# Longer rows for gates and values in memory, and loads asked for one stage ahead, in a two-layer attention kernel

## The reference, cut to what matters

```python
def _mixer_swa(h, positions, w_in, sinks):
    proj = h @ w_in
    q, k, v, z = jnp.split(proj, [MIX_WIDTH, MIX_WIDTH + SWA_KV, MIX_WIDTH + 2 * SWA_KV], axis=-1)
    q = _rope(q.reshape(B, S, N_HEADS, HEAD_DIM), positions)
    k = _rope(k.reshape(B, S, SWA_KV_HEADS, HEAD_DIM), positions)
    o = _banded_gqa(q, k, v, SWA_WINDOW, sinks).reshape(B, S, MIX_WIDTH)
    return o * jax.nn.silu(z)

def _mixer_mla(h, positions, w_in, q_norm, kv_norm, w_uq, w_ukv):
    cq, ckv, kr, z = jnp.split(h @ w_in, [...], axis=-1)
    q = (_rmsnorm(cq, q_norm) @ w_uq)      # nope 64 and rope 32 per head
    kv = (_rmsnorm(ckv, kv_norm) @ w_ukv)  # key 64 and value 64 per head
    o = _mla_attention(q_nope, q_rope, k_nope, k_rope, v)
    return o * jax.nn.silu(z)

for i in range(DEPTH):
    y = mixers[i % N_MIXERS](x, ...) @ w_out[i]
    x = _layernorm(DEEPNORM_ALPHA * x + y, ln_g[i], ln_b[i])
    x = x + jax.nn.sigmoid(x @ pe_gate[i]) * (p[i] @ pe_proj[i])
```

## Time and profile before

| what | value |
|---|---|
| median of 3 runs | 3186.99 us (3185.19 to 3197.34) |
| the profiled execution, its own time | 3190.66 us |
| its span | 3188.8 us |
| mean granted TensorE clock | 0.968 |
| PE busy | 2962.2 us (93%) |
| DVE, ACT, POOL busy | 1895.7, 1627.8, 1430.5 us |
| DMA packets, bytes | 311302, 540.87 MB |

### The profile page before, as it was taken

How to read it: one execution, slowest core, us unless ns; L and a number is a source line. 1 busy time by engine, 2 the same in 40 slices (tenths; PEclk the granted TensorE clock), 3 DMA queues, 4 the chain that set the end, 5 groups by cost and what they waited for, 6 DMA issues and landing times. The chain is left out here.

```text
span 3188.8 us, 40986 instructions
## 1 busy us (share of the span) xinstructions
PE 2962.2 (93%) x13536; PEld 2324.3 (73%) x13536; DVE 1895.7 (59%) x2696; ACT 1627.8 (51%) x2830; POOL 1430.5 (45%) x1154
## 2 busy tenths in 40 slices
PE   7999977887999999999987599999999999799998
PEld 6888875565788788777765377777777777588876
DVE  3544213443378864555653478787787787347875
ACT  3111213566435544444554177777777777544553
POOL 0022003555222540000653078888888888522353
PEclk9999998999999999999999599999999999899999
DMA  5255339885997675554899832432533432499674
GB/s 171 77 121 128 109 92 203 181 178 136 286 289 242 211 241 181 172 169 157 292 355 322 220 72 70 101 98 71 128 71 89 108 72 54 120 307 282 226 233 151
DMA packets 311302, 540.87 MB, mean 170 GB/s; under 512 B 48000, under 2 KB 135680, under 8 KB 302912
## 3 DMA queue, kind: packets, MB, share of 16 engines
q1 hardware_dynamic: 222176, 387.82, 43.5%
q10 hardware_dynamic: 88928, 150.64, 15.7%
HBM read 361.79 MB, written 176.29 MB: 169 GB/s over the span
## 5 line engine op out<-in xcount | busy, mean ns | idle before, releaser
L2454 POOL TENSOR_TENSOR mla_pl<-mla_p,mla_ph 128x512 fp32r<-128x512 f32 (+3 forms) x640 | 707.2, 1120 | 205.4 <-ACT mla_p L2325 197.7
L1455 PE MATMUL end_bank<-end_xh,end_whi 128*128 128x512 f32 x1808 | 719.0, 398 | 61.4 <-DVE end_xl L1706 28.7
L1456 PE MATMUL end_bank<-end_xl,end_whi 128*128 128x512 f32 x1808 | 708.4, 392 | 0.0
L1457 PE MATMUL end_bank<-end_xh,end_wlo 128*128 128x512 f32 x1808 | 707.8, 391 | 0.0
L2175 PE MATMUL mla_score<-mla_q,mla_k 96*128 96x512 f32 (+7 forms) x1920 | 555.2, 391 | 5.0 <-DMA mla_q<-mla_m_t 5.0
L1528 ACT CAST end_whi<-end_wraw 128x1024 fp32r<-128x1024 f32 (+1 forms) x228 | 234.1, 1027 | 599.6 <-PE end_bank L1457 516.6
L2324 ACT ACTIVATE mla_ph<-mla_score 128x512 fp32r<-128x512 f32 (+3 forms) x640 | 341.3, 533 | 223.3 <-PE mla_score L2175 219.9
L1692 DVE TENSOR_TENSOR end_wlo<-end_wraw,end_whi 128x1024 fp32r<-128x1024 f32 x188 | 254.5, 1353 | 337.2 <-ACT end_whi L1528 337.2
L1455 PEld LDWEIGHTS end_bank<-end_xh,end_whi 128*128 128x128 f32 x1808 | 342.5, 189 | 152.8 <-issue 35.1
L2175 PEld LDWEIGHTS mla_score<-mla_q,mla_k 96*128 96x128 f32 (+1 forms) x1920 | 362.3, 193 | 90.1 <-issue 35.5
L2355 DVE TENSOR_REDUCE mla_mx<-mla_mx 128x1 f32<-128x512 f32 (+3 forms) x640 | 372.3, 604 | 93.3 <-PE mla_mx L2175 92.5
(11 more groups left out here) (211 smaller groups left out, 4566.4 us busy)
## 6 DMA issues: line engine op xcount, KB each, us to landing
end_wraw<-in_w_out ACTq DMA_DIRECT2D x64, 512.0 KB, 7.7
end_wraw<-in_pe_gate ACTq DMA_DIRECT2D x64, 512.0 KB, 5.0
end_wraw<-in_w_in ACTq DMA_DIRECT2D x56, 512.0 KB, 3.8
swa_q<-scratch_q_hi SPq DMA_DIRECT2D x32, 512.0 KB, 12.3
end_raw<-scratch_o SPq DMA_DIRECT2D x32, 512.0 KB, 11.2
end_factor<-scratch_inv SPq DMA_DIRECT2D x64, 256.0 KB, 9.6
scratch_proj<-end_out_f SPq DMA_DIRECT2D x64, 256.0 KB, 6.7
scratch_sum<-end_out_f SPq DMA_DIRECT2D x64, 256.0 KB, 6.3
```

What stands on the lines that cost most here:

```text
L1455: nc.tensor.matmul(bank, wh[:, at], xh[:, k0 + k, :], start=(k == 0), stop=False)
L1456: nc.tensor.matmul(bank, wh[:, at], xl[:, k0 + k, :], start=False, stop=False)
L1457: last = nc.tensor.matmul(bank, wl[:, at], xh[:, k0 + k, :], start=False, stop=(k == kc - 1))
L2454: pool.tensor_tensor(p_lo[b][:, off:TC], prob[b][:, off:TC], p_hi[b][:, off:TC].bitcast(F32), ALU.subtract).then_inc(p_lo_ok, 1)
```

## The change

- **Gates of layer 0.** `z0` becomes [4, 16, 64, 4, 128]. A gate load is 64 rows of 2 KB. A store of `in0` becomes two DMAs of 64 partitions with rows of 512 bytes.
- **Values of layer 0.** `v0` becomes [4, 128, 16, 256]: high, ones, low and zeros for each token and head. POOL writes the ones and zeros once, after the last rotation, into output tiles that lie in the cosine table. A store has rows of 1 KB and twice the bytes; `swa` fetches one tile in place of two, 8 or 9 KB in a row for each partition, and the memsets L2345 and L2346 are gone.
- **Values of layer 1.** `v1` becomes [2, 128, 16, 1024]. A store of `ukv` has rows of 4 KB, a load of `mla` rows of 512 bytes.
- **Closings.** The four pieces of `p` and the first three weight blocks are issued by SP at the end of the attention block before, after its last loads, into tiles that live across blocks.
- **First queries and keys of `mla`.** The five loads of `load_high(0)` (1.3 MB) are issued in `end0`, four tiles before its end, after waits for the stores that they read; they stand in SP's queue ahead of the last five value stores.
- **Both attention blocks.** SP waits for the first unit's maxima to have landed (`mrow[0]`) before it issues `load_high(2)` and `load_low(1)`.

```diff
-            v_out = [s.sb(f"vout{b}", [P, v_heads, v_group, 2, HEAD_DIM], F32R) for b in range(2)]
+            v_out = [cos[:, b * SEQ // 2:(b + 1) * SEQ // 2].bitcast(F32R).rearrange(
+                "p (h g part d) -> p h g part d", h=v_heads, g=1, d=HEAD_DIM) for b in range(2)]
...
                             sp.wait_ge(sems["ready"], n + 1)
+                            if kind == "silu":
+                                heads = arg["dst"].rearrange("g c d j t -> g j d c t")
+                                for e in range(2):
+                                    sp.dma_start(heads[li, 2 * b + e, :, t * GROUP:(t + 1) * GROUP, :],
+                                                 out_f[t % 2][e * HEAD_DIM:(e + 1) * HEAD_DIM, :].rearrange(
+                                                     "d (c t) -> d c t", t=P)).then_inc(sems[f"stored{t % 2}"], 16)
+                                continue
...
+            if v:
+                pool.wait_ge(seg_sems[last_rope]["steps"], 4 * NTC * segments[last_rope][1])
+                for tile in v_out:
+                    pool.memset(tile[:, :, :, 1, :].bitcast(F32), 1.0)
+                    op = pool.memset(tile[:, :, :, 3, :].bitcast(F32), 0.0)
+                op.then_inc(v_filled, 1)
...
                 elif kind == "v":
-                    sp.dma_start(latent["v"][x["i"] * 8:(x["i"] + 1) * 8, :, 4 * q + x["at"], :].rearrange(
-                        "h p d -> p h d"), v_tile(n).rearrange("p h two d -> p h (two d)")
-                        ).then_inc(v_stored[values[n] % 3], 16)
+                    sp.dma_start(latent["v"][x["i"], :, 4 * q + x["at"], :], v_tile(n).rearrange(
+                        "p h two d -> p (h two d)")).then_inc(v_stored[values[n] % 3], 16)
...
-            for n in range(4):
-                load_piece(n)
...
+                if latent and n == total - 4:
+                    for m in range(first[-2], first[-2] + 8):
+                        wait_stored(sp, m)
+                    for b in range(2):
+                        sp.wait_ge(turn_stored[b], 16 * len(turn_tiles))
...
+                    latent["first_loads"](sp)
...
-            for b in range(n_raw):
-                load_block(b)
...
-            load_high(0)
+            if not here:
+                load_high(0)
             load_low(0)
             load_high(1)
             for c in range(len(chunks)):
                 u = chunks[c][0]
                 if c == 0 or chunks[c - 1][0] != u:
+                    if c == 0:
+                        sp.wait_ge(mrow[0], 16)
                     if u + 2 < units:
                         load_high(u + 2)
                     if u + 1 < units:
                         load_low(u + 1)
+            cfg["next_loads"](sp)
...
-        for tile, at in ((vals, 0), (vals_lo, HEAD_DIM)):
-            yield tile[:, 0:n // P, 0:HEAD_DIM], v[g, :, t0 // P:(t0 + n) // P, at:at + HEAD_DIM]
+        yield vals[:, 0:n // P, :], v[g, :, t0 // P:(t0 + n) // P, :]
...
-                gate_src=lambda u, c: heads(gates, u, c), dst=lambda u, c: heads(out, u, c),
+                gate_src=lambda u, c: gates[u // 2, u % 2 * half_b + c], dst=lambda u, c: heads(out, u, c),
...
-        yield vals[:], v[u]
+        half_heads = HEADS // 2
+        yield vals[:], v[u // half_heads].rearrange("p n (h d) -> h p n d", d=P)[u % half_heads]
...
+            def loads(sp):
+                pieces = a[f"p{layer}"].rearrange("(k p) t -> p k t", p=P)
+                for n in range(NTC):
+                    sp.dma_start(early["raw"][:, 2 * n:2 * n + 2, :], pieces[:, :, n * TC:(n + 1) * TC]
+                                 ).then_inc(early["x_in"][n], 16)
+                for g in range(2):
+                    sp.dma_start(early["w_raw"][g][:].rearrange("p (i c) -> p i c", i=4),
+                                 a[f"pe_proj{layer}"][4 * g:4 * g + 4].rearrange("i p c -> p i c")
+                                 ).then_inc(early["w_in"][g], 16)
+                sp.dma_start(early["w_raw"][2][:], a[f"w_out{layer}_0"][0]).then_inc(early["w_in"][2], 16)
```

More of the change, by code:

```diff
@@ L335, in stores_of @@
                 return [(sems[f"stored{b}"], 64 * n) for b in range(2)]
-            return [(sems[f"stored{b}"], 16 * NTC // 2 * n * (1 if kind == "gate" else 2)) for b in range(2)]
+            each = {"gate": 1, "silu": 4}.get(kind, 2)
+            return [(sems[f"stored{b}"], 16 * NTC // 2 * n * each) for b in range(2)]
         tables_at = tables["at"] if making else next(
@@ L1192, in chain_phase @@
         stat_ps = [s.ps(f"stat{r}", [P, TC]) for r in range(2)]
-        w_in = [s.sem(f"w_in{b}") for b in range(n_raw)]
-        x_in = [s.sem(f"x_in{b}") for b in range(8)]
+        w_in, x_in = early["w_in"], early["x_in"]
         old_in = [s.sem(f"old_in{b}") for b in range(n_old)]
@@ L1400, in _ @@
                     store(m)
+                if latent and n == total - 4:
[3 more added lines that the diff above has]
+                        sp.wait_ge(turn_stored[b], 16 * len(turn_tiles))
+                    for m in range(first[jobs.index(("in", NTC - 1))], first[jobs.index(("in", NTC - 1)) + 1]):
+                        if tiles[m]["kind"] == "kr":
+                            wait_stored(sp, m)
+                    latent["first_loads"](sp)
                 x = tiles[n] if n < total else None
@@ L2343, in _ @@
                 op = vec.memset(tile[rows:kr, :].bitcast(F32), 1.0)
-            for b in range(0 if long else 2):
-                vec.memset(vals[b][:, :, HEAD_DIM:P].bitcast(F32), 1.0)
-                op = vec.memset(vals_lo[b][:, :, HEAD_DIM:P].bitcast(F32), 0.0)
             op.then_inc(const_ok, 1)
```

111 lines of the change are left out of this document (64 added, 47 removed).

## The result

The changed kernel takes 3169.97 us (median of 5, 3161.16 to 3172.56) where the kernel before takes 3190.79 (median of 5): a ratio of 0.9927, 95% interval 0.9912 to 0.9941. It is 21 us faster, not the 49.5 us of the forecast, and outside its range. The profiled executions took 3190.66 and 3169.97 us, so the two traces differ by just the amount to be explained (their spans by 20.7 us).

A forecast was written before the change was run, and what follows sets the result against it. PE was taken as busy for 93% of the span, its long waits lying where blocks meet and where DMA is full. The terms -14.1 - 15 + 0.5 - 3 - 11 - 4 - 2.9 gave -49.5 us: 3138 us, range 3120 to 3149.

The forecast's parts named there:

- Closings, -14.1: Both closings: with pieces and weights loaded early, PE starts 6.75 and 6.38 us sooner; -14.1 us, bounds -9 and -18.
- Rival 5: Closings and start of `mla`: early loads do nothing because blocks start late; 3156 us, chance 0.04.
- `swa`'s steady state, -15: Units of `swa`: fewer gate rows beside a full q1 win 15 of 24 us excess; bounds 3 and 24.
- Rival 1: `swa`: rows are not a turn's cost, or output stores alone set the stall; -15 becomes -2, 3151 us, chance 0.13.
- Start of `swa`, -3: Start of `swa`: fewer gate packets beside the first keys, and first maxima sooner, 1.5 us each; bounds 0 and -6.
- just in time: Start of `swa`: the held-back 5.2 MB take 25 us, due when unit 1 starts some 27 to 30 us later.
- `ukv`, -11: `ukv`: longer rows make 32 value stores cheaper by 14.7 us, of which 11 taken; bounds 4 and 17.
- second rival: `ukv` is bound by bytes and key tiles, and early queries push stores out; -15 becomes -3, 3150 us, chance 0.11.
- Early loads of `mla`, -4: Start of `mla`: 10.1 us of load wait goes, up to 6.4 comes back through late stores; bounds 0 and -9.
- -2.9 for the maxima: Start of `mla`: with q1 empty the first maxima DMA lands in 1.8 us; -2.9 us, bounds -1 and -3.5.
- Rival 3: `mla`: the 512-byte loads come onto the path for all 41 us; 3179 us, chance 0.05.
- rival 4: `swa`: SP's wait for the maxima starts a queue that never catches up; 3229 us at 45 us a unit, chance 0.03.

The follow-up runs named there:

- late_close: The changed kernel with the seven loads of each closing issued by SP at the closing's start, not a block ahead: 3184.80 us, ratio 0.9973.
- v_short: The changed kernel with `swa` loading its values again in two transfers of 256-byte rows, gates still in long rows: 3149.53 us, ratio 0.9874.
- no_wait_swa: The changed kernel without SP's wait for the first maxima in `swa`, kept in `mla`: 3163.34 us, ratio 0.9917.
- v1_old: The changed kernel with `mla`'s values tensor as before, so `ukv` stores 512-byte rows and `mla` reads 8 KB rows: 3175.92 us, ratio 0.9944.
- late_first: The changed kernel with `mla`'s first queries and keys asked for when `mla` begins, as before: 3165.91 us, ratio 0.9927.
- v_six: The changed kernel with six value tiles in `ukv` instead of three: 3151.26 us, ratio 0.9873.
- ones_pool: The changed kernel with `mla`'s three rows of ones filled by POOL instead of DVE: 3159.83 us, ratio 0.9894.
- gate_old: The changed kernel with the gates' tensor as before, 256 rows of 512 bytes a chunk, values still in long rows: 3178.50 us, ratio 0.9963.
- v_1k: The changed kernel with `swa`'s values, same bytes, in rows of 1 KB instead of 8 or 9 KB: 3149.19 us, ratio 0.9850.
- best2: The changed kernel with `swa`'s values in 1 KB rows and output in 2 KB rows, and `mla`'s ones filled by POOL: 3133.33 us, ratio 0.9824.

## Why the prediction was right and wrong

**Closings, -14.1: right, in mechanism and size.** PE's idle time before them fell from 15.14 and 13.54 us to 8.41 and 7.18, by 6.73 and 6.36; the forecast had 6.75 and 6.38. The fold and what follows gained 1.7 us in the first closing and 1.5 in the second instead of 1 each, and late_close is 14.8 us slower. Rival 5 fails.

**`swa`'s steady state, -15: the step that failed.** The mechanism (turns on an engine, so many rows of q10 beside a full q1) was right, and 15.5 us of gain for the gates, by v_short, is the 15 of the forecast. That agreement is partly luck: the working gave all 24, and 15 was a choice between bounds of 3 and 24. What failed is the sentence on the values, "A gain of 0 to 3 us of transfer a unit, in the 24 us already". It priced the long rows as bytes and rows on their own queue, and did not carry the turn's price over to them. The forecast took 0.26 us as what a q1 packet costs; it held for queries and keys only. While values were read, q1's packets cost 0.042 us and q10 caught up there: 702 of its packets beside 1511 in 5 us, from 556 us on in the kernel before:

```profile
q1 hardware_dynamic: 1511, 0.83, 80.6%
q10 hardware_dynamic: 702, 0.33, 33.3%
```

With rows of 8 and 9 KB a turn costs 0.44 us instead, and 15.1 us were lost again (16.4 beside short gate queues, by v_short). The bound of -3 did not hold either, since it allowed no loss. Rival 1 named the outcome, not the cause. Units stayed at 36.9 us, the prediction's own sign of failing. Of its other signs, "landings of gates near 3 us" failed with it: their median is 7.8 us, where it was 4.7 before.

**Start of `swa`, -3: wrong in sign, +2.0.** PE's wait for the first keys stayed (21.2 us). To the first score 1.2 us were gained, but not by SP's wait, since no_wait_swa has them too. Then unit 0 took 29.3 us from first score to maxima DMA instead of 26.2, with PE waiting 2.3 us for an output buffer. The step that failed is "just in time": it asked whether the held-back loads arrive, not what they do to the stores beside them. Without the wait, or with shorter value rows, the loss is gone.

**`ukv`, -11: right within its bounds, 9.4 by v1_old, 8.9 between the kernel before and late_first without the maxima's DMA.** "The stage is full of transfers, so nearly all of it should come through" was still not the whole of it: PE and three value tiles form a loop through the landing of a store, and v_six shows that this loop was worth half as much again (14.0 us against 9.4). Of the second rival one half fails: the stage was not bound by its bytes, at 347 GB/s with 396 to be had. The other half came true: the early queries push the stores out by 7 us.

**Early loads of `mla`, -4: wrong, no gain and a loss of up to 2.7; -2.9 for the maxima: right, -2.6.** Two parts of the -4 were right, the wait hidden (10.9 us, forecast 10.1) and what comes back through the stores (7.2, forecast up to 6.4). The third was put at nothing because nobody asked what DVE did during the load wait: filling the rows of ones, 5.9 us, which ones_pool wins back.

**`mla`, 0: +3.4.** No transfer costs it; the clock does, as the last section tells. Rival 3 fails, and so does rival 4: SP's wait costs 2.9 us once, not in every unit.

So of the 28.8 us missing, 15.9 are in `swa`'s units, 5.0 at its start, 8.5 from `ukv` to the first score of `mla` (some 6 in the early loads, 2 in the rows), and 3.4 in the clock, less 4.0 us of small gains.

## What to carry to other kernels

When two queues share the engines, a row's length on the one is the other's waiting time: count (rows of the queue that is late) times (cost of a row of the queue that is full), for every kind of row that the full queue carries, and lengthen rows on the late queue first. The Trainium skill (Perfetto Trace Analysis, DMA Optimizations) warns of DMAs under 2 KB and would batch them to 4 or 8 KB. It speaks of whole DMAs; taken for rows, as the prediction took it, it agrees with the stores of `ukv`, but in `swa` rows of 1 KB and of 256 bytes beat rows of 8 KB by 15.4 and 16.4 us over five units, since their reading was hidden and what they delayed was not. Before a wait is removed, list what every other engine does under it; and where a stage is full by its share and also shows waits for a buffer's landing, try more buffers as well as cheaper transfers.

## What was not expected of the hardware

**When the clock comes back.** In `mla` TensorE's granted clock was 0.50 (1.2 GHz) from PE's idle time on, through the first maxima (in ones_pool PE was busy for 27.12 of 34 us there), and rose to 1.00 (2.4 GHz) only some time after the scores had made PE fully busy. That time falls into two groups over the profiles: 10.2 to 13.2 us in ten of them (the kernel before among them, 13.1), and 19.0 to 19.5 us in five (the changed kernel, gate_old, v_1k, late_close, best2). The scores take 914.4 to 916.1 us in the first kind and 918.5 to 919.8 in the second: 4 us, which are in the changed kernel's profile. No edit separates the two kinds in an evident way, but each kernel has one profile, so that one kernel takes both is not shown. What is on record is that the mean clock of v_1k's four executions runs from 0.970, the profiled one, to 0.976. The Trainium skill (TensorE: Matmul & The Clock Gate, Part 1) says that the moment of the rise differs from run to run, by some half a microsecond either way; the traces agree that it differs, but by up to 9 us between kernels.

**A turn is a row.** Beside rows of 7.9 KB on q1, q10 moved exactly as many rows of 0.5 KB, 62 and 62. With q1's rows at 1 KB the counts are equal from 596 us (314 and 313) but not from 598 (569 and 231), and q10's stores still take 7.6 us to land; why q10 falls behind there is not settled.
